# Memory attention's products as three fp32r products each, and the output products of two self-attentions spread around their last head pair

## The reference, cut to what matters

```python
def causal_block_attention(q, k, v, scale, log_f_cum=None): ...   # softmax attention, 16 heads

def fox_attention(xn, w_in, b_f, w_o):
    ...
    return o.reshape(B, S, FOX_WIDTH) @ w_o

def mla_attention(xn, positions, k, v, w_dq, cq_norm, w_uq, w_o):
    c_q = rmsnorm(xn @ w_dq, cq_norm)
    q = (c_q @ w_uq).reshape(B, S, MLA_HEADS, MLA_NOPE + MLA_ROPE)
    ...
    return o.reshape(B, S, MLA_HEADS * MLA_V) @ w_o

def memory_cross_attention(hn, mn, w_cq, w_ckv, w_co):
    q = (hn @ w_cq).reshape(B, S, X_HEADS, X_HEAD_DIM)
    k, v = jnp.split(mn @ w_ckv, 2, axis=-1)
    ...
    s = jnp.einsum('bshd,bmhd->bhsm', q, k) * (X_HEAD_DIM ** -0.5)
    p = jax.nn.softmax(s, axis=-1)
    o = jnp.einsum('bhsm,bmhd->bshd', p, v).reshape(B, S, D_MODEL)
    return o @ w_co
```

## Time and profile before

| | us |
|---|---|
| median of 3 runs (1858.59 to 1864.25) | 1859.72 |
| the profiled execution | 1863.09 |
| its span, first to last instruction | 1860.6 |
| TensorE busy | 1672.8 (90% of the span) |
| VectorE busy | 1030.1 (55%) |
| ACT busy | 529.4 (28%) |
| GpSimd busy | 347.6 (19%) |

### The profile page before, as it was taken

How to read it: one execution, slowest core, us unless ns; L and a number is a source line. 1 busy time by engine, 2 the same in 40 slices (tenths; PEclk the granted TensorE clock), 3 DMA queues, 4 the chain that set the end, 5 groups by cost and what they waited for, 6 DMA issues and landing times.

```text
span 1860.6 us, 22203 instructions
## 1 busy us (share of the span) xinstructions
PE 1672.8 (90%) x7627; PEld 1169.8 (63%) x7627; DVE 1030.1 (55%) x2419; ACT 529.4 (28%) x1077; POOL 347.6 (19%) x296
## 2 busy tenths in 40 slices
PE   6999999989999998999999999788887977888877
PEld 5888999858679996785665685544343433344333
DVE  6555555533255554456544111676676777766775
ACT  2544444313334442324210111122222212212122
POOL 4550000000000000000000000344434443343540
PEclk9999999999999998999999999999989989898989
DMA  6534566312545662432404340599999999999997
GB/s 205 182 91 138 180 188 195 130 40 82 172 143 174 188 206 69 133 117 91 181 23 179 138 145 28 208 420 421 421 422 421 421 421 421 421 421 421 421 421 304
DMA packets 205765, 437.38 MB, mean 235 GB/s; under 512 B 10608, under 2 KB 136976, under 8 KB 171792
## 3 DMA queue, kind: packets, MB, share of 16 engines
q0 software_dynamic: 36864, 268.45, 34.7%
q1 hardware_dynamic: 168848, 168.20, 28.1%
HBM read 435.54 MB, written 1.05 MB: 235 GB/s over the span
## 4 chain that ended last, share of the span: by engine, by line
PE 72%; DMA 16%; DVE 7%; issue 3%; ACT 1%; SPq 0%; POOL 0%; DVEq 0%; ACTq 0%
PE ps L527 34%; DMA OT<-in_peer_uv,IX 13%; PE ps L1399 12%; PE ps L726 6%; PE ps L1188 3%; PE ps L1045 3%; PE ps L1058 3%; PE ps L701 2%; PE ps L558 2%; PE ps L603 2%; DMA SLOT<-in_peer_uv,IX 2%; DVE SLOT L2623 1%; PE ps L533 1%; DMA SLOT<-in_w_uq_by_pair 1%; PE ps L1137 1%
## 5 line engine op out<-in xcount | busy, mean ns | idle before, releaser
L1853 POOL DMA_INDIRECT SLOT<-in_peer_uv,IX x128 | 137.3, 1073 | 1309.8 <-DVE IX L2617 1065.2
L1399 PE MATMUL ps<-SLOT,AR 128*128 128x512 f32 x512 | 267.5, 679 | 92.9 <-ACT AR L1771 92.9
L1399 PEld LDWEIGHTS ps<-SLOT,AR 128*128 128x128 f32 x512 | 109.6, 219 | 244.5 <-issue 132.3
L527 PEld LDWEIGHTS ps<-ARH 128*128 128x128 f32 x1920 | 233.0, 192 | 1.6
L527 PE MATMUL ps<-ARH 128*128 128x256 f32 x1920 | 233.5, 283 | 0.0
L2623 DVE SCALAR_TENSOR_TENSOR SLOT<-SLOT,V 128x1024 f32<-128x1024 f32 x128 | 153.3, 1224 | 78.2 <-DMA SLOT<-in_peer_uv,IX 76.2
L1987 DVE TENSOR_TENSOR ARH<-SLOT,ARH 128x2048 fp32r<-128x2048 f32 (+1 forms) x88 | 154.1, 1756 | 48.0 <-ACT ARH L1482 31.2
L1399 PE MATMUL ps<-AR 128*128 128x512 f32 x320 | 144.3, 600 | 10.1 <-ACT AR L1771 10.1
L726 PE MATMUL ps<-ARH 128*128 128x512 f32 x528 | 123.9, 390 | 0.0
L1765 ACT ACTIVATE AR<-AR 128x4 f32<-128x4 f32 (+1 forms) x66 | 13.5, 205 | 381.9 <-DVE SLOT L2623 187.2
L1399 PEld LDWEIGHTS ps<-AR 128*128 128x128 f32 x320 | 60.0, 191 | 83.2 <-issue 64.1
(11 more groups left out here) (416 smaller groups left out, 2519.6 us busy)
## 6 DMA issues: line engine op xcount, KB each, us to landing
SLOT<-in_w_gate SPq DMA_DIRECT2D x44, 512.0 KB, 4.0
SLOT<-in_w_up SPq DMA_DIRECT2D x44, 512.0 KB, 5.3
SLOT<-in_w_down SPq DMA_DIRECT2D x44, 512.0 KB, 5.6
SLOT<-in_w_in SPq DMA_DIRECT2D x9, 2048.0 KB, 8.8
SLOT<-in_fox_w_in SPq DMA_DIRECT2D x16, 512.0 KB, 5.3
SLOT<-in_w_ckv SPq DMA_DIRECT2D x4, 2048.0 KB, 8.1
XT<-in_w_pq_by_head SPq DMA_DIRECT2D x8, 1024.0 KB
SLOT<-in_w_uq_by_pair SPq DMA_DIRECT2D x8, 768.0 KB
```

Source lines behind the costliest of these rows:

```text
L527: m = pe.matmul(outp, l, r, start=(n_ == 0), stop=(n_ == len(pairs) - 1))
L1399: m = pe.matmul(ps[:, b, :], DIAG[:, j, :], v_row(j)[:, c * 512:(c + 1) * 512], start=False, stop=closing)
L1853: pool.indirect_dma_start(PAIR[j], None, pairs, bass.IndirectOffsetOnAxis(IX[:, t, j:j + 1], 0)).then_inc(gathered[j], 16)
```

## The change

- **Memory attention.** The eight chunk pairs and the four value banks are done as three fp32r products. ACT casts the high halves (`high_columns`, `high_chunks`: twelve casts of 128x2048, and those of the two normalised inputs), VectorE subtracts (`low_columns`, `low_chunks`, in place in the slot). The high halves lie in parts of the arena that are free then, and in `OT` and `XT`. TensorE waits for `split[s]` instead of `here[s]`. ACT's root for the queries' norm moves ahead of the third key copy, and `mixed(1)` on VectorE comes behind four subtractions.
- **Attention loops.** In both attentions `turn` stands before the first `mix_values`.
- **Last pair.** The output product is cut in parts: seven products (fox: eight parts of three) before `attend`, the other ready ones behind it, then `turn`, then pair 6's share, then pair 7's.
- **MLA's second pair.** Its query weights go to slot 2, loaded ahead.
- **Start.** The 2 MB load of slot 2 comes after the ten gains.

```diff
         MEM = arena(8228, NT, D)
-        XM = arena(10276, KC, S)
+        XMHL = (halves(10276, KC, S), halves(8228, KC, S))
         KALL, QALL = arena(12324, KC, S), arena(14372, KC, S)
         PALL, PTALL = arena(0, NT, D), arena(2048, NT, KC, P)
         DGM = arena(3072, NT, P)
         MSCR = arena(13348, NT, D)
+        KQ_HIGH = [halves(at, KC, S) for at in (4096, 6144, 0, 2048)]
+        V_HIGH = [halves(4096, 4, 512), halves(6144, 4, 512)]
+        V_HIGH += [x[:].rearrange("p a b -> p (a b)").rearrange("p (a b) -> p a b", a=4) for x in (OTR, XTR)]
...
+        def columns(x, g):
+            return view(x[:], KC, 512)[:, :, g % 2 * S:g % 2 * S + S]
+        def chunks(x, q):
+            return view(x[:], KC, 512)[:, 4 * q:4 * q + 4, :]
...
-            def two_tiles(w, c0=0):
+            def two_tiles(w, c0=0, arrival=here):
                 for c in range(2):
-                    fill(2 + c, (slot(2 + c, KC, 512), rows(w, c0 + 512 * c, c0 + 512 * c + 512)))
+                    fill(2 + c, (slot(2 + c, KC, 512), rows(w, c0 + 512 * c, c0 + 512 * c + 512)), arrival=arrival)
             def ffn(l):
...
             sp.dma_start(H[:], x_in).then_inc(sem("x_here"), 16)
-            fill(2, (slot(2, KC, 512), rows(fw, 2048, 2560)))
             for name, src in GAINS:
                 r0 = g_at[name]
                 sp.dma_start(SLOT[0][r0:r0 + src.shape[0], 0:P], src).then_inc(here[0], 16)
             T.add(used[0])
+            fill(2, (slot(2, KC, 512), rows(fw, 2048, 2560)))
...
             qk(rows(w_uq, 0, 2 * P), w_uk[:, :, 0:P])
-            with T.loop("mla", PAIRS - 1) as i:
-                kq(dyn(w_uq, i * 2 * P + 2 * P, 2 * P), w_uk[:, :, ds(i * P + P, P)])
+            fill(2, (slot(2, QR // P, 2 * P), rows(w_uq, 2 * P, 4 * P)))
+            fill(1, (slot(1, 2, P), w_uk[:, :, P:2 * P]))
+            with T.loop("mla", PAIRS - 2) as i:
+                kq(dyn(w_uq, i * 2 * P + 4 * P, 2 * P), w_uk[:, :, ds(i * P + 2 * P, P)])
...
             for c0 in (0, D):
                 for s_ in range(2):
-                    fill(s_, (slot(s_, KC, 512), rows(wckv, c0 + 512 * s_, c0 + 512 * s_ + 512)))
-                two_tiles((wcq, a["w_co_2"][0])[c0 // D])
+                    fill(s_, (slot(s_, KC, 512), rows(wckv, c0 + 512 * s_, c0 + 512 * s_ + 512)), arrival=raw_here)
+                if c0 == 0:
+                    two_tiles(wcq, arrival=raw_here)
...
-            def out_begin(ready):
-                pe.wait_ge(here[2], T.next(here[2], 16))
-                for t in range(NT):
+            def out_part(t, ks):
+                if ks[0] == 0:
                     take(6 + t)
-                    for k in range(ready):
-                        first(pe.matmul(ps[:, 6 + t, :], cols(OT, t, k), slot(2, KC, 512)[:, k, :], start=(k == 0), stop=False))
-            def out_end(ready, bank):
-                evacuated(bank)
-                for t in range(NT):
-                    for k in range(ready, KC):
-                        m = pe.matmul(ps[:, 6 + t, :], cols(OT, t, k), slot(2, KC, 512)[:, k, :], start=False, stop=(k == KC - 1))
+                for k in ks:
+                    m = pe.matmul(ps[:, 6 + t, :], cols(OT, t, k), slot(2, KC, 512)[:, k, :], start=(k == 0), stop=(k == KC - 1))
+                    if k < KC - 1:
+                        first(m)
+                if ks[-1] == KC - 1:
                     m.then_inc(full["v"][6 + t], 1)
                     T.add(free["v"][6 + t])
-                release(2)
-                row_tile(3, (2, 3), OT)
             def qk_part(s_):
...
...
-                mix_values(i, 0)
                 if turn_before:
                     turn()
+                mix_values(i, 0)
                 mix_values(i, 1)
...
-                mix_values(i, 0)
                 if i:
                     fox_turn()
+                mix_values(i, 0)
                 mix_values(i, 1)
...
-            for t, b in ((0, 6), (1, 0)):
-                take(b)
-                for n_, (l_, r_) in enumerate(tile_thirds(OTHL, t, 2, range(PAIRS - 2))):
-                    first(pe.matmul(ps[:, b, :], l_, r_, start=(n_ == 0), stop=False))
+            def fox_out(t, ks):
+                b = (6, 0)[t]
+                if ks[0] == 0:
+                    take(b)
+                for k in ks:
+                    for n_, (l_, r_) in enumerate(tile_thirds(OTHL, t, 2, [k])):
+                        m = pe.matmul(ps[:, b, :], l_, r_, start=(k == 0 and n_ == 0), stop=(k == KC - 1 and n_ == 2))
+                        if k < KC - 1:
+                            first(m)
+                if ks[-1] == KC - 1:
+                    m.then_inc(full["v"][b], 1)
+                    T.add(free["v"][b])
+            fox_out(0, range(PAIRS - 2))
+            fox_out(1, range(2))
             fox_attend(PAIRS - 1)
+            fox_out(1, range(2, PAIRS - 2))
             fox_turn()
+            fox_out(0, [PAIRS - 2])
+            fox_out(1, [PAIRS - 2])
             evacuated(7)
-            for t, b in ((0, 6), (1, 0)):
-                pairs = tile_thirds(OTHL, t, 2, range(PAIRS - 2, KC))
-                for n_, (l_, r_) in enumerate(pairs):
-                    m = pe.matmul(ps[:, b, :], l_, r_, start=False, stop=(n_ == len(pairs) - 1))
-                m.then_inc(full["v"][b], 1)
-                T.add(free["v"][b])
+            fox_out(0, [KC - 1])
+            fox_out(1, [KC - 1])
             release(2)
             row_thirds(3, (2, 3), OTHL, 4, loads=2)
...
             release(3)
             turned(KVA, 6, (0, 1, 2))
...
-            def mla_proj(grown=False):
+            def mla_proj(grown=False, s=0):
                 pe.wait_ge(here[1], T.next(here[1], 16))
                 take(6)
                 group(ps[:, 6, 0:S], ((slot(1, 2, P)[:, k, :], CKT[:, k, :]) for k in range(2))).then_inc(full["a"][6], 1)
                 release(1)
                 T.add(free["a"][6])
-                pe.wait_ge(here[0], T.next(here[0], 16))
+                pe.wait_ge(here[s], T.next(here[s], 16))
                 take(0)
                 for hh in range(2):
-                    pairs = [[(slot(0, 6, 2 * P)[:, k, P * hh:P * hh + P], CQT[:, k, :])] for k in range(6)]
+                    pairs = [[(slot(s, 6, 2 * P)[:, k, P * hh:P * hh + P], CQT[:, k, :])] for k in range(6)]
                     m = grown_group(ps[:, 0, hh * S:(hh + 1) * S], pairs) if grown else group(ps[:, 0, hh * S:(hh + 1) * S], sum(pairs, []))
-                release(0)
+                release(s)
                 m.then_inc(full["v"][0], 1)
                 T.add(free["v"][0])
...
             evacuated(4, 5, 6, 7)
             mla_scores(0)
...
-            mla_proj()
+            mla_proj(s=2)
             attend(0, turn_before=False)
             assert not pending
...
             mla_scores(PAIRS - 1)
-            out_begin(PAIRS - 2)
+            pe.wait_ge(here[2], T.next(here[2], 16))
+            out_part(0, range(PAIRS - 2))
+            out_part(1, range(1))
             attend(PAIRS - 1)
+            out_part(1, range(1, PAIRS - 2))
             turn()
-            out_end(PAIRS - 2, 2)
+            for t in range(NT):
+                out_part(t, [PAIRS - 2])
+            evacuated(2)
+            for t in range(NT):
+                out_part(t, [KC - 1])
+            release(2)
+            row_tile(3, (2, 3), OT)
             ffn(1)
...
             def chunk_pair(X, s_, g, b):
+                pe.wait_ge(split[s_], T.next(split[s_]))
                 take(b)
+                w = (KQ_HIGH[g], columns(SLOTR[s_], g))
                 for c in range(2):
-                    n_ = (2 * g + c) % 4
-                    m = group(ps[:, b, c * S:(c + 1) * S], ((slot(s_, KC, 512)[:, k, n_ * P:(n_ + 1) * P], X[:, k, :]) for k in range(KC)))
+                    m = group(ps[:, b, c * S:(c + 1) * S], sum((thirds(lambda h: w[h][:, k, c * P:(c + 1) * P], lambda h: X[h][:, k, :]) for k in range(KC)), []))
                 m.then_inc(full["a"][b], 1)
                 T.add(free["a"][b])
...
...
                 take(b)
-                group(ps[:, b, :], ((cols(XM, t, k), slot(c, KC, 512)[:, k, :]) for k in range(KC))).then_inc(full["v"][b], 1)
+                if t == 0:
+                    pe.wait_ge(split[c], T.next(split[c], 2))
+                w = (lambda k: V_HIGH[2 * c + k // 4][:, k % 4, :], lambda k: low_of(c, KC, 512)[:, k, :])
+                group(ps[:, b, :], sum((thirds(lambda h: cols(XMHL[h], t, k), lambda h: w[h](k)) for k in range(KC)), [])).then_inc(full["v"][b], 1)
...
-            turned(MEM, KC, (4, 5, 6, 7), reader="a", freer="a", scale=DGM)
...
-                if g % 2 == 0:
-                    pe.wait_ge(here[g // 2], T.next(here[g // 2], 16))
                 if g == 3:
-                    turned(H, KC, (0, 1, 2, 3))
-                chunk_pair(XM, g // 2, g, 4 + g)
+                    turned(H, KC, (0, 1, 2, 3), reader="a")
+                chunk_pair(XMHL, g // 2, g, 4 + g)
```

(73 more changed lines are left out.)

## The result

The changed kernel took 1832.12 us (median of 4 executions, 1828.57 to 1833.56), the kernel before beside it 1860.35: ratio 0.9846, 95% interval 0.9825 to 0.9866. That is 28.2 us less; the prediction was 33.8 less, 1826, range 1818 to 1837. The profiled execution took 1833.39 us (span 1831.3).

What follows compares the result with a forecast made beforehand. Before 1,180 us TensorE with its waits was taken to bound the kernel, behind that the expert gather's DMA. Seven terms summed to 33.8 us, taken off the 1859.7 median: 1826 us, range 1818 to 1837.

Steps and rivals of the forecast that it cites:

- memory attention: Memory attention: fp32r thirds for key and query pairs 10.0, value banks 5.1, no wait for the root 1.3; 16.4 us saved.
- turn before the mix, fox: Fox attention's middle pairs: the turn's two transposes moved into TensorE's wait for ACT's copy; 1.4 us saved.
- turn before the mix, latent (whole loop): Latent attention loop: the same move, counted for five rounds because of the weights' load; 1.15 us saved, bounds 0 and 1.4.
- last pair, fox: Fox attention's last pair: 14.4 us instead of 18.74; 4.3 us saved, 1.7 of it clock, bounds 2.6 and 4.6.
- last pair, latent: Latent attention's last pair: 16.6 us instead of 21.68; 5.1 us saved, bounds 1.9 (clock still low) and 5.3.
- second pair, latent: Latent attention's second pair: query weights loaded ahead into slot 2; 3.5 us saved, between 0.1 (half clock) and 5.3 (full).
- start: Kernel start: gain rows no longer queue behind a 2 MB load; 1.9 us saved, bounds 0 and 3.2.
- rival 3: The clock stays low where its return was counted, or falls elsewhere: 1831 to 1835 us, chance 0.11.
- rival 2: Memory attention: a split half arrives late, stalls of 5 to 10 us give 1831 to 1836 us, chance 0.14.
- rival 4: Memory attention: three fp32r products don't run at the fox's rate, nothing of the 15.1 us, 1841 us, chance 0.03.
- rival 5: Memory attention: casts and subtractions not hidden; all twelve exposed are 50 us, giving 1876 us, slower; chance 0.03.
- rival 6: Last stage: doesn't pass the upstream gain on, as if started by something other than the indices; 1859 us, chance 0.01.

Runs made afterwards that it cites:

- the doubled products: The changed kernel with the merged branches' output products done twice in both token tiles, just before the memory attention: 1858.08 us, ratio to the kernel before 0.9993.

## Why the prediction came out as it did

The result is in the range and 6 us above the point. By its own steps, the stretches of the two first profiles against each other:

| step | predicted | measured | three profiles each |
|---|---|---|---|
| memory attention | 16.4 | 16.4 | 16.4 |
| turn before the mix, fox | 1.4 | 1.0 | 0.9 |
| turn before the mix, latent (whole loop) | 1.15 | 1.4 | 1.2 |
| last pair, fox | 4.3 | 4.6 | 4.9 |
| last pair, latent | 5.1 | 5.2 | 4.7 |
| second pair, latent | 3.5 | 5.2 | 4.7 |
| start | 1.9 | 2.6 | 1.4 |
| sum | 33.8 | 36.4 | 34.1 |

That the sum meets 34.1 (added before rounding) is partly luck: the second pair and fox's last pair were 1.8 us too low together, and three smaller terms 1.4 too high.

- **Memory attention: right in its three parts.** Pairs of 5.75 us (17.25 / 3), value banks under the transposes' cover, no wait for the root. The 12 casts and subtractions cost TensorE nothing, and a second set of four doesn't either, in its profile.
- **Second pair: undersized.** The point between the bounds was a guess on the clock. It stayed full in all ten profiles with the new attentions (6.31 us for 28 instructions each time, against 7.66 for 24), so the upper bound held. An idle time of 1.1 to 1.3 us, for the key weights, still stands in front (1.51 before); the one that is gone is that for the query load (2.58 us).
- **Latent loop: the right sum from a wrong place.** I had each of five rounds shorter by the two transposes. No steady round got shorter, since the load into the slot just read takes the place of the wait; the 1.4 us are in the first round and the last. The prediction names this load, and bounds the term by 0; in the steady rounds 0 was the value.
- **Start: right within the spread.** The first fox pair's projection began at 45.8 to 47.5 us in the nine profiles with the new order of loads and at 47.3 to 49.9 in the five with the old one, means 46.6 and 48.5: 1.9 us. What the prediction sized wrong is its lower case, a gain of 0.5: it let each of the four subtractions wait out a cast of 128x2048 (27.4 to 39.8, 3.1 us each, which is 1.22 and 1.90). VectorE and GpSimd at that place (timeline):
```profile
27.04 2.04 POOL L1881 CAST ARH<-SLOT 128x1024 fp32r<-128x1024 f32 x1
28.09 2.06 DVE L2042 TENSOR_TENSOR SLOT_R<-SLOT,ARH 128x1024 fp32r<-128x1024 f32 x1
...
31.00 2.89 POOL L1895 CAST ARH<-SLOT 128x2048 fp32r<-128x2048 f32 x1
...
32.05 2.91 DVE L2042 TENSOR_TENSOR SLOT_R<-SLOT,ARH 128x1024 fp32r<-128x1024 f32 x1
```

Alone a subtraction takes 1.22 us, a cast of 128x1024 1.04 and one of 128x2048 1.90. Side by side they alternate: three subtractions of 2.03 to 2.06 us beside small casts and one of 2.91 beside a large one, 8.82 in all; in the kernel before two of the four met large casts, 9.36. Each pair falls 0.2 us short of the sum of its two times alone. The rule of the Trainium skill ("SBUF — State Buffer", SBUF: two separate sides), that one of the two waits out the other's whole instruction, agrees with this trace to that 0.2 us.

- **The base.** The sum was made in a profiled execution of 1863.1 us, which lay 1.9 above the mean of all 41, and it was taken off a median of three, 1859.7, which lay 1.5 below it. And it took the rest of the program for unchanged. In the profile that came with the result U2 was 5.0 us longer than in the profile of before; repeats of the same kernel put it at 533.4 and 533.9. Among the signs of being wrong the prediction names "a new low-clock stretch [...] behind the shortened parts". One stood there, by chance, in that execution.
- **What is left.** Edited stretches give 34.1 us over three profiles each. The times give 30.5 (29.2 to 31.8). 2.7 of the 3.6 between them are the unedited stretches of the same six profiles, mostly the one U2. Over all profiles the unedited stretches lean the same way: U2 takes 534.3 us on average in nine with the new attentions (the run that edits it left out, and the added 27.5 us of the doubled products taken off) and 532.9 in four with the old ones, U3 715.9 in ten with the new memory attention and 715.1 in four with the old one. That is some 2 us together, of which some 1 us is the stretch at 826 us that two of the nine profiles have. So few profiles do not tell a lasting loss from chance, and the comparisons themselves gave 29.3 to 32.3 us: it stays open. The executions without a trace, which carry the means, can't be cut up.

Of the rivals, rival 3 gives the time that was first measured (1831 to 1835), but only by half of its mechanism: the clock came back wherever I counted on it, and fell elsewhere, which the rival also names, in one execution. The two repeats have no such stretch, and their medians, 1829.9 and 1829.8, lie in the forecast's own 1820 to 1831. Rivals 2, 4, 5 and 6 are refuted by the chain without waits, the 48 instructions in 5.75 us, the idle VectorE, and the doubled products.

## What to carry to other kernels

Before an order is changed in a loop, look for the second chain of the same length: here load, projection, release ran 10.58 us beside a chain of 10.55 through TensorE and ACT's copy, and only removing both gained anything in a steady round, by the profiles. A block that TensorE works through while another engine uses an early result is a cover; to interleave it for another reason can cost a wait and then the clock behind it. Take the sum of stretches against several executions, not one: here unedited code differed by up to 6.5 us between profiles of the same length of work, and a sum from rows was within 1 us of the edited places over three profiles each (within 3 in the two first) while the time missed by 6.

## What the hardware showed beyond that

- With TensorE busy without a gap in both, the same products ran at 0.50 for 6.8 us in one execution and at 1.00 in another. A clock read off one profile is one draw.
- After an idle time of 1.98 us that an experiment made, the granted clock was 0.50 for 3.4 us, and the next eight instructions took 5.41 us (3.45 without the wait). An idle time of 1.1 to 1.3 us in front of the latent attention's second pair had no such stretch behind it in any of ten profiles.
- A VectorE subtraction of 128x1024 with two SBUF inputs takes 1.22 us alone, 2.05 beside GpSimd casts of 128x1024 and 2.91 beside one of 128x2048: the two engines take turns by whole instructions, but for 0.2 us each time.
